# One decoder layer on one core: the down-projection partly in 2x2 blocks with seven products

## What is computed

```python
def swiglu(h, w_gate, w_up, w_down):
    return (jax.nn.silu(h @ w_gate) * (h @ w_up)) @ w_down

xp = xp + swiglu(rmsnorm(xp, norm_ffn[l]), w_gate[l], w_up[l], w_down[l])
y = rmsnorm(x, norm_final)
```

## Time and profile before

| | us |
|---|---|
| median of 3 runs | 807.65 (806.68 to 808.87) |
| profiled execution, first to last instruction | 805.9 |
| PE busy | 765.7 (95%) |
| DVE busy | 551.7 (68%) |
| ACT busy | 380.6 (47%) |
| POOL busy | 126.7 (16%) |

### The profile page before, as it was taken

The page is one execution under the profiler, slowest core; times in us unless marked ns, Lnnn a source line. Parts: engine busy times, 40 slices in busy tenths (PEclk is TensorE's granted clock), DMA queues, the critical chain, the costliest instruction groups (busy, mean ns, idle before and its releaser), DMA issues. The chain is left out here.

```text
span 805.9 us, 16038 instructions
## 1 busy us (share of the span) xinstructions
PE 765.7 (95%) x6308; PEld 732.2 (91%) x6308; DVE 551.7 (68%) x1103; ACT 380.6 (47%) x826; POOL 126.7 (16%) x179
## 2 busy tenths in 40 slices
PE   5999998898999998799999999999999999999995
PEld 5999887874899998788899999999999999999995
DVE  5778665677466699656388899888888878223323
ACT  5524775522264333755344375555555557212313
POOL 0376303331005821000046000000000000000000
PEclk9999999999999999999999999999999999999998
DMA  9413333453587578994333313333333323432312
GB/s 269 110 54 95 94 104 131 157 189 125 173 299 243 172 202 244 311 337 138 98 106 94 101 53 106 105 105 106 105 106 106 105 73 88 135 92 83 89 47 106
DMA packets 142192, 109.93 MB, mean 136 GB/s; under 512 B 9255, under 2 KB 134144, under 8 KB 139039
## 3 DMA queue, kind: packets, MB, share of 16 engines
q1 hardware_dynamic: 135255, 90.32, 36.7%
q0 software_dynamic: 3104, 14.68, 5.5%
q10 hardware_dynamic: 3760, 3.92, 1.4%
HBM read 103.93 MB, written 5.20 MB: 135 GB/s over the span
## 5 line engine op out<-in xcount | busy, mean ns | idle before, releaser
L1766 DVE TENSOR_TENSOR wlo<-wraw,whi 128x512 fp32r<-128x512 f32 (+1 forms) x207 | 145.6, 744 | 97.5 <-ACT whi L1144 91.3
L1144 ACT ACTIVATE whi<-wraw 128x512 fp32r<-128x512 f32 (+1 forms) x186 | 103.6, 608 | 127.2 <-PE ps L2556 74.2
L2554 PE MATMUL ps<-B_hi,whi 128*128 128x260 f32 x384 | 110.0, 286 | 3.5 <-DVE xT L1811 1.6
L2556 PE MATMUL ps<-B_hi,wlo 128*128 128x260 f32 x384 | 108.5, 282 | 0.0
L2555 PE MATMUL ps<-B_lo,whi 128*128 128x260 f32 x384 | 108.4, 282 | 0.0
L2555 PE MATMUL ps<-h_lo,whi 128*128 128x260 f32 x352 | 99.6, 283 | 0.0
L2554 PE MATMUL ps<-h_hi,whi 128*128 128x260 f32 x352 | 99.5, 283 | 0.0
L2556 PE MATMUL ps<-h_hi,wlo 128*128 128x260 f32 x352 | 99.4, 282 | 0.0
L2554 PE MATMUL ps<-A_hi,whi 128*128 128x260 f32 x264 | 76.5, 290 | 0.3 <-ACT kn_lo L1238 0.3
L2554 PEld LDWEIGHTS ps<-B_hi,whi 128*128 128x128 f32 x384 | 72.3, 188 | 4.7 <-DVE xT L1811 1.8
L2555 PE MATMUL ps<-A_lo,whi 128*128 128x260 f32 x264 | 75.2, 285 | 0.0
(11 more groups left out here) (489 smaller groups left out, 2082.1 us busy)
## 6 DMA issues: line engine op xcount, KB each, us to landing
kv_slot<-in_cache_mem_k_dram SPq DMA_DIRECT2D x8, 1024.0 KB, 8.7
kv_slot<-in_cache_mem_v_dram SPq DMA_DIRECT2D x8, 1024.0 KB, 6.9
wraw<-in_w_down_dram SPq DMA_DIRECT2D x16, 512.0 KB
wraw<-in_w_out_dram SPq DMA_DIRECT2D x14, 512.0 KB
wraw<-in_w_up_dram SPq DMA_DIRECT2D x12, 512.0 KB, 4.5
xraw<-in_w_gate_dram SPq DMA_DIRECT2D x20, 256.0 KB, 3.6
xraw<-in_w_up_dram SPq DMA_DIRECT2D x10, 512.0 KB, 4.1
wraw<-in_w_in_dram SPq DMA_DIRECT2D x9, 512.0 KB
```

Of the source, the lines that this page charges most:

```text
L1144: act.activation(whi[:, home(s), c0:c1], wraw[:, s % RAW, c0:c1], ACT.Copy).then_inc(w_hi, 1)
L1766: return dve.tensor_tensor(dst, src, high.bitcast(F32), ALU.subtract)
L2554: pe.matmul(dst, left[0], right[0], start=first, stop=False)
L2556: return pe.matmul(dst, left[1], right[0], start=False, stop=last)
```

## The change

The first 6 of the 22 input chunks of the down-projection stay plain (`NPLAIN`); 16 are done in 2x2 blocks in two parts of 8 chunks. The work is numbered on from the gate/up units: j = 22 to 25 are plain pairs of output tiles (pieces C0 to C3, 3 chunks each, 384 columns), j = 26 to 29 (`U_A` on) the four pairs of output tiles for part 0, j = 30 to 33 (`U_B` to `U_LAST`) for part 1. The last unit, 33, has eight plain products. The pieces go around the same ring of 8 as those of the gate/up units, and the weights come through the same two raw buffers and `load_b`; the slots of w_down are gone.

Of h, only chunks 0 to 5 are split one by one. For each part the operands are quarters [128, 4, 260] of `h_raw` ("11", "12", "22", in part 1 also "21") and four sums S1 to S4 of them, each with a high part by ACT and a low part by DVE, 1040 columns. The sums are made by POOL (`hidden_sums`), for both parts, from the end of the last gate/up product on; DVE makes no low part of part p before all four sums of p are made. POOL also makes the 1024 wide difference of each blocked unit, and adds the three snapshots of each unit to `xT` (260 columns), where DVE adds the four banks. In its loop DVE makes T2(j+1) after the low of B22(j), `fourth_added(j-1)` and `corner_added(j-1)`. The end of the final norm is put in another order: the four rows of products of the last unit alternate with the turns of group 0 and then of group 1.

```diff
-    for m in range(KD - 1):
-        o += [("d", m, f) for f in (0, 1)]
...
+    o += [("d", m, f) for m in range(KD) for f in (0, 1)]
+    for j in range(U_A, U_LAST):
+        o += [("sx", j), ("sy", j), ("sz", j)]
...
+            def hidden_sums(p):
+
+                of = D_OF[p]
+                a11, a12, a21, a22 = (of[n][2] for n in ("11", "12", "21", "22"))
+                s1, s2, s3, s4 = (of[n][2] for n in ("S1", "S2", "S3", "S4"))
+                gp.wait_ge(val, VAL["h", chunks_of(p)[1][1] - 1] + 1)
+                for n, (dst, x, y, op) in enumerate(((s1, a21, a22, ALU.add), (s2, s1, a11, ALU.subtract),
+                                                     (s3, a11, a21, ALU.subtract), (s4, a12, s2, ALU.subtract))):
+                    gp.tensor_tensor(dst, x, y, op).then_inc(h_summed, 1)
+                    gp.wait_ge(h_summed, 4 * p + n + 1)
+
+            def differences(j):
+
+                gp.wait_ge(b_loaded[(j - J0) % 2], 48 * ((j - J0) // 2 + 1))
+                gp.wait_ge(piece_lo, PIECE["T3", NF - 1 if j == U_A else j - 1] + 1)
+                r = braw[(j - J0) % 2]
+                gp.tensor_tensor(t13[:, :], r[:, 2 * WB:4 * WB], r[:, WB:3 * WB], ALU.subtract).then_inc(t13_made, 1)
+
+            def add_snap(j, n, m, f, src, prior):
+
+                c0, c1 = HALF[f]
+                gp.wait_ge(snap, snaps_before(j) + n)
+                gp.wait_ge(val, VAL[prior] + 1)
+                gp.tensor_tensor(xT[:, m, c0:c1], xT[:, m, c0:c1], src, ALU.add).then_inc(snap_added, 1)
+
+            multiplied(gp, "B22", NF - 1)
+            hidden_sums(0)
+            hidden_sums(1)
+            differences(U_A)
+            for j in range(U_A, U_LAST):
+                if j + 1 < U_LAST:
+                    differences(j + 1)
+                m0, m1 = tiles_of(j)
+                g, u, first = gate[j % 2], upv[j % 2], j < U_B
+                add_snap(j, 1, m0, 0, g[:, 0:TH], ("xd", m0, 0) if first else ("g0", j - 4))
+                add_snap(j, 2, m1, 0, u[:, 0:TH], ("xd", m1, 0) if first else ("u0", j - 4))
+                add_snap(j, 3, m1, 1, u[:, TH:T], ("u1", j))
...
+            NEXT_HIGH = {U_A: ("S1", "S2"), U_A + 1: ("S3", "12"), U_A + 2: ("22", "S4")}
+            for j in range(U_A, U_LAST):
...
+                piece_high("B11", j + 1)
...
+                shot(g[:, 0:TH], "B11", 1)
+                piece_high("B22", j)
+                if more:
+                    piece_high("T2", j + 1)
+                shot(u[:, 0:TH], "T2", 2)
+                if more:
+                    piece_high("T1", j + 1)
+                    piece_high("T3", j + 1)
...
+                shot(u[:, TH:T], "T3", 3)
+                for name in ("B21", "T4") if more else ("B12", "B22"):
+                    piece_high(name, j + 1)
...
+                for name in NEXT_HIGH.get(j, ()):
+                    operand_high(1, name)
...
+            def operand_low(p, name):
+
+                dve.wait_ge(h_summed, 4 * (p + 1))
+                high, low_, raw = D_OF[p][name]
+                low(("D", p, name), low_, raw, high)
...
+            for j in range(U_PLAIN, U_A - 1):
+                m0, m1 = tiles_of(j)
+                piece_low("C0", j + 1)
+                piece_low("C1", j + 1)
+                if j == U_PLAIN + 1:
+                    operand_low(0, "11")
+                    operand_low(0, "12")
+                elif j == U_PLAIN + 2:
+                    operand_low(0, "S1")
+                    operand_low(0, "S2")
+                plain_added(m0)
+                piece_low("C2", j + 1)
+                piece_low("C3", j + 1)
+                if j == U_PLAIN + 1:
+                    operand_low(0, "22")
+                elif j == U_PLAIN + 2:
+                    operand_low(0, "S3")
+                plain_added(m1)
+            piece_low("B11", U_A)
+            mixed_corner(U_A)
+            last_corner(U_A)
+            piece_low("T2", U_A)
+            operand_low(0, "S4")
+            piece_low("T1", U_A)
+            plain_added(KD - 2)
+            piece_low("T3", U_A)
+            operand_low(1, "11")
+            piece_low("B21", U_A)
+            plain_added(KD - 1)
+            piece_low("T4", U_A)
...
+            for j in range(U_A, U_LAST):
+                more = j + 1 < U_LAST
+                piece_low("B11", j + 1)
+                piece_low("B22", j)
+                if j > U_A:
+                    fourth_added(j - 1)
+                    corner_added(j - 1)
+                if more:
+                    mixed_corner(j + 1)
+                    piece_low("T2", j + 1)
+                    last_corner(j + 1)
+                    piece_low("T1", j + 1)
+                    piece_low("T3", j + 1)
+                else:
+                    piece_low("B21", j + 1)
+                first_added(j)
+                for name in ("B21", "T4") if more else ("B12", "B22"):
+                    piece_low(name, j + 1)
+                second_added(j)
+                for name in NEXT_LOW.get(j, ()):
+                    operand_low(1, name)
...
+            for j in range(U_A, U_LAST):
+                x = out(("sx", j))
+                mul(x, "B11", j, operand(j, "11"), True)
+                if j > U_A:
+                    down_corner(j - 1)
+                copied_out(j, 1)
+                mul(x, "T2", j, operand(j, "S2"), False)
+                y = out(("sy", j))
+                mul(y, "T1", j, operand(j, "S1"), True)
+                copied_out(j, 2)
+                mul(x, "T3", j, operand(j, "S3"), False)
+                z = out(("sz", j))
+                mul(z, "B21", j, operand(j, "12"), True)
+                copied_out(j, 3)
+                mul(x, "T4", j, operand(j, "22"), False)
```

More of the change, by code:

```diff
@@ L550, in build @@
         where["at"] = a0
-        h_hi = keep("h_hi", [NF, T], F32R)
+        h_hi = keep("h_hi", [NPLAIN, T], F32R)
+        where["at"] = a0 + NF * RB
         h_lo = keep("h_lo", [NF, T], F32R)
@@ L2501, in _, with last_added @@
-            for g, ts in enumerate(Y_GROUP):
-                add_residual(("d", KD - 1, g), ("xo3", KD - 1, g), KD - 1, g)
-                dve.wait_ge(y_sq, 10 + ts[-1] + 1)
+            def last_added(m, f):
+                if (m, f) == (KD - 1, 1):
+                    dve.wait_ge(snap_added, 3 * (U_B - 1 - U_A) + 3)
+                else:
+                    own((("g0", "x4")[f] if m == KD - 2 else "u0", U_B - 1))
+                if f:
+                    b = full(dve, ("e", m, 1))
+                else:
+                    multiplied(dve, ("B21", "B22")[m - KD + 2], U_LAST)
+                    b = bank(("e", m, 0))
+                add_to(("xo3", m, f), m, f, b)
@@ new lines, in last_product @@
+            def last_product(b, name, left, first):
+                pe.wait_ge(piece_lo, PIECE[name, U_LAST] + 1)
+                w_h, w_l = piece_at(name, U_LAST)
+                for k in range(4):
+                    c = slice(k * P, (k + 1) * P)
+                    ins = mm3(b[:, 0:TH], (w_h[:, c], w_l[:, c]), (left[0][:, k, :], left[1][:, k, :]),
+                              first and k == 0, not first and k == 3)
+                return ins
+            last = {name: operand(U_LAST, name) for name in ("11", "12", "21", "22")}
@@ new lines, in _ @@
+            b = out(("e", KD - 2, 0))
+            last_product(b, "B11", last["11"], True).then_inc(product, 1)
+            down_corner(U_LAST - 1)
+            last_product(b, "B21", last["12"], False).then_inc(product, 1)
+            after(("u0", U_LAST - 2))
+            pe.wait_ge(snap_added, 3 * (U_LAST - 1 - U_A))
+            for t in range(5):
+                turn_rows(("y", t, 0), t, range(4))
+            b = out(("e", KD - 1, 0))
+            last_product(b, "B12", last["11"], True).then_inc(product, 1)
@@ new lines, in _ @@
+            last_product(b, "B22", last["12"], False).then_inc(product, 1)
+            b = out(("e", KD - 2, 1))
+            last_product(b, "B11", last["21"], True)
+            filled(last_product(b, "B21", last["22"], False), ("e", KD - 2, 1))
+            after(("xo3", KD - 1, 0))
+            pe.wait_ge(snap_added, 3 * (U_LAST - U_A))
+            for t in Y_GROUP[0]:
+                turn_rows(("y", t, 1), t, range(4, KD))
+            b = out(("e", KD - 1, 1))
+            last_product(b, "B12", last["21"], True)
@@ new lines, in _ @@
+            after(("xo3", KD - 2, 1))
+            for t in Y_GROUP[1]:
+                turn_rows(("y", t, 1), t, range(4, KD - 1))
+            filled(last_product(b, "B22", last["22"], False), ("e", KD - 1, 1))
+            after(("xo3", KD - 1, 1))
+            b = out(("z", 1))
+            for i, t in enumerate(Y_GROUP[1]):
+                n, c = rows_of(t), t * P
+                ins = pe.transpose(b[0:n, i * P:(i + 1) * P], xT[:, KD - 1, c:c + n], ident[:, :])
+            filled(ins, ("z", 1))
```

439 lines of the change are left out of this document (275 added, 164 removed).

## The result

| kernel | median us (range, runs) | ratio to before [95%] | profiled span | of it the down-projection and the end |
|---|---|---|---|---|
| before | 808.26 (806.68 to 809.38, 4) | | 805.9 | 139.6 |
| after | 824.57 (823.46 to 825.61, 4) | 1.0209 [1.0187, 1.023] | 823.6 | 155.6 |

The kernel became slower by 16.3 us, where 8.7 was forecast: the sign is right, the size is about half, and the time lies 2.6 above the range. The last column runs from the start of the first matmul of the down-projection (666.29 before, 667.96 after) to the end of the span. It grew by 16.0.

What follows compares the result with a forecast made beforehand. PE, 95% busy, was taken as the bound by instruction count: -10.1 (84 matmuls) + 8.9 (start) + 9.1 (rounds) + 0.8 (later units) = +8.7, so 816.4 us. Forecast's own range 809 to 821; with part of a rival, 801 to 822.

Steps and rivals of the forecast that it cites:

- C2 of pair 2: Piece of the third plain pair: ready at 23.7 us, due at 22.4, so PE waits 1.3.
- The start: From the down-projection's start to T3 of the first blocked unit: 8.9 us lost to plain waits, first snapshot and T3.
- the cycle of a sum and a low: Plain part: POOL's eight sums run with one DVE low between two, 2.0 + 0.45 each, 20 us in all.
- The first snapshot: ACT's first copy of a product in the first blocked unit: 0.7 us that nothing hides.
- T3's wait: PE before T3 of the first blocked unit, waiting for ACT's copy behind DVE's late T2: 6.1 us.
- The rounds: Three blocked units with two big lows: DVE's round 13.1 us against PE's 10.07, 3.0 lost each, 9.1 in all.
- the first rival: Little contention: POOL's work falls into DVE's waits, big-low rounds are 10.7, total 800.4 us; chance 0.17.
- POOL's part: In a big-low unit, POOL adds 2.0 + 3 x 0.5 = 3.5 us to DVE's round, some 0.1 falling in DVE's waits.
- Two units without big lows: Later blocked units: DVE's round 10.9 us but partly in its waits, so 0.4 lost in each, 0.8 together.
- The tail: Work behind the last matmul: same chain as before, cost 0, or +1 if the PE products covering it are thin.
- The second: Rival: contention only in the sums, start costs 8.9, units 1 in all, total 807.5 us; chance 0.09.
- The third: Rival: full blocking, each POOL instruction costs DVE its whole time, 0.3 more each, total 825 us; chance 0.08.

Runs made afterwards that it cites:

- e1_pool_short: Changed kernel with all 36 POOL instructions of the change (sums, differences, adds) cut to one column, that work left out of the result: 802.79 us.
- e2: Changed kernel with only POOL's 8 sums cut to one column; differences and adds stay whole: 815.14 us.
- e3: Changed kernel with only POOL's 7 differences and 21 adds cut to one column; the 8 sums stay whole: 808.21 us.
- e12: Changed kernel with only POOL's 7 differences cut to one column; 8 sums and 21 adds stay whole: 811.39 us.
- e10_fill: Changed kernel with extra matmuls into an unused bank ahead of PE's wait before T3 in the first four blocked units: 824.23 us.
- e6_all_dve: Changed kernel with sums, differences and adds all moved from POOL to DVE, nothing left out: 812.53 us.
- e4_copy_first: Changed kernel with ACT copying out a unit's T2 product before making the high part of the next T2: 820.31 us.
- e5_diff_dve: Changed kernel with the 7 differences moved to the head of DVE's round; sums and adds stay on POOL: 823.15 us.
- e7_all_dve_copy_first: e6_all_dve with ACT copying out a unit's T2 product before making the high part of the next T2: 807.13 us.

## Why the prediction was right in sign and short in size

**Right.** The saving: 84 matmuls fewer. The mechanism: DVE and POOL taking turns, confirmed by taking POOL's work away (e1_pool_short) in three portions (e2, e3, e12). The place: before T3, through ACT's high part of the next T2 and the copy behind it; and C2 of pair 2 as the largest plain wait, 1.1 where 1.3 was forecast.

**The start, forecast 8.9, measured 11.05.** The step that failed is the cycle of a sum and a low. The prediction took 2.0 + 0.45 = 2.45; it is 2.70, eight times 2 us later. POOL's price was taken at 2.3 and is 2.43 clean, and DVE's low costs it 0.25 on top. The plain part therefore lost 4.3 instead of 2.1: not by the last wait but by six small ones of 0.2 to 0.4 before it, each with about 0.26 for the restart. The prediction had 0.8 for all of these. The first snapshot cost 1.8 instead of 0.7. Its wait is 1.48 in the changed kernel and 0.54 without the differences (e12_diffs_short, e3_units_short), but also 0.54 with the differences and without the sums (e2_sums_short): the excess needs both, and was charged to neither. T3's wait, forecast 6.1, was 5.0; that part of the delay had been taken earlier fits this, but no run separates it.

**The rounds, forecast 13.1, measured 14.2.** The term was made of two parts, and both were wrong, in opposite ways. DVE's round without POOL was taken as 9.7, hidden under 10.07; it is 10.8 (e1_pool_short, e3_units_short), which was the first rival's chain, T4's low waiting for PE's product and the lows and adds behind it. POOL's part was taken as 3.5, of which 0.1 was to fall into DVE's waits. In the round it is 0.70 for three adds (taken as 1.5) and 1.5 to 1.9 for the difference (13.05 to 13.44 in e10_fill less 11.52, taken as 2.0): 2.5 together. The price of an add was not far off (DVE's rows are 1.3 longer by three); DVE's waits took up more than the 0.1. 10.8 + 2.5 = 13.3, near 13.1 by luck. The remaining 0.9 per unit is the clock, the second step that failed, which wasn't a term of the sum at all: waits near 3 us were forecast, and the 0.120 was read where the granted clock was 1.00. Three rounds lost 12.3 instead of 9.1.

**Two units without big lows, forecast 0.8, measured 2.1.** POOL's work was credited to DVE's waits; in e12_diffs_short, with the adds alone, these units lose 0.2 together (10.18 and 10.14), so it is the difference that doesn't find room.

**The tail, forecast 0 (+1 if its cover is thin), measured 0.6.** The chain has a DVE row of the first group ahead of the last add, where it had none. It stands with the same wait of 1.1 in all twelve experiments, none of which took the row away, so this is read, not shown.

**The sum.** 8.9 + 9.1 + 0.8 + 0 stands against 11.05 + 12.3 + 2.1 + 0.6 (with 0.1 before the tail). Of the 7.4 missing, 2.2 lie in the start, 3.2 in the rounds (2.7 of it the clock), 1.3 in the later units, 0.6 in the tail and 0.1 before it. The range failed because its upper end moved only POOL's price (0.3 each), not the slow clock or the restart of a waiting PE.

**The rivals.** The first (little contention, 800.4) is what e1_pool_short measures, 802.8: its working was sound and its condition false. The second falls with e12_diffs_short: leaving out the differences alone gains 13.7. The third (full blocking) named 825, and the time is 824.6, but not for its reason: it charges POOL's whole time, and the rows show 2.2 lost to a sum of 2.43, and 0.55, 0.24 and 0.54 to adds of 260, which take 0.62 to 0.83 with DVE nearly quiet. The rule of the Trainium skill's "SBUF — State Buffer", section "SBUF: two separate sides", that the loser is blocked for the whole instruction holds for the big ones to about a tenth; an add costs DVE's row 0.1 to 0.6 less than the add's own time, and the round less still, since DVE waits in it anyway.

**Still open:** how much of the median the clock takes (0 to 3 us by e10_fill); why the wait of 2.40 us before 760.38 was followed by no fall where one of 1.88 was; why the first snapshot waits longer only with sums and differences together; and the tail.

## What to carry to other kernels

An idle GpSimd is not free room for work that VectorE can do: where both read two SBUF operands, as here, one waits for the other, and the move costs VectorE nearly GpSimd's time (2.2 of 2.43 us for 1040 elements) in place of its own (1.2). Compare VectorE's rows beside such an instruction with those without one before moving anything. Then count the round of every engine with its waits in it, not its busy time: here VectorE's work, added up as 9.1, was a round of 10.8 before any contention, and copies that TensorE awaits belong ahead of work that waits for a late engine.

## What the runs showed of the hardware

- Waits of TensorE of 4.80, 1.88 and 2.19 us were followed by 3 to 5 us with a granted clock of 0.55 to 0.57 on average, a matmul every 0.22 us instead of 0.12; the one of 2.40 and those of 1.48 and less weren't. The other kernels show the same overlap: a fall behind waits of 3.68 (e6_all_dve), 3.52 and 3.08 (e4_copy_first), 3.03 and 3.06 (e2_sums_short), 2.14 (e5_diff_dve) and 1.83 (e7_all_dve_copy_first), none behind 2.51 (e2_sums_short) and 1.92 (e3_units_short, e12_diffs_short). So the length of the wait alone doesn't decide it. With matmuls in the gap (e10_fill) the clock stayed at 1.00.
- Who goes first between VectorE and GpSimd isn't fixed. Beside the sums every low waited, one to a sum. The first difference was itself held up: it took 4.26 us beside two lows of 384, one of 1040 (1.22, its clean time) and two adds from PSUM, before the next low was made to wait (2.21). What decides it no run shows.

```profile
699.93 4.26 POOL L1223 TENSOR_TENSOR t<-wraw 128x1024 f32<-128x1024 f32 x1 [10.15 <-issue]
```

```profile
700.71 1.22 DVE L1946 TENSOR_TENSOR h_lo<-h_raw,D_hi_S 128x1040 fp32r<-128x1040 f32 x1
...
702.54 2.21 DVE L1946 TENSOR_TENSOR wlo<-wraw,whi 128x512 fp32r<-128x512 f32 x1
```
